# Shared expert rows added to the residual in DRAM during routing; the last stage loads two ranks at a time and adds two on VectorE

## The reference

```python
gate_w = ROUTED_SCALE * sel / sel.sum(-1, keepdims=True)      # top 8 of 64 experts per token
# each expert: (silu(xb @ Wg[e]) * (xb @ Wu[e])) @ Wd[e], on blocks of 128 (token, rank) pairs
routed = segment_sum(yb * row_w)                              # sum of the 8 ranks of a token
shared = (silu(t @ Sg) * (t @ Su)) @ w_shared_down
x = layer_norm(ALPHA * x1 + gate * (routed + shared)) * ln2_g + ln2_b
```

## Time and profile before

| what | value |
|---|---|
| median of 3 runs | 2107.01 us (2103.72 to 2113.51) |
| profiled execution | 2111.06 us |
| its span, first to last instruction | 2109.3 us |
| mean granted TensorE clock | 0.96 |
| PE busy | 1990.6 us, 94% |
| DVE busy | 1127.3 us, 53% |
| POOL busy | 541.9 us, 26% |

### The profile page before, as it was taken

One profiled execution on the slowest core, in us unless ns is written; L12 is line 12 of the kernel. 1 busy time (PEld: TensorE's weight loads), 2 busy tenths in 40 slices (PEclk: granted clock), 3 DMA queues, 4 the chain that ended last, 5 costly groups with the idle time before them and its releaser, 6 DMA issues. The chain is left out here.

```text
span 2109.3 us, 34455 instructions
## 1 busy us (share of the span) xinstructions
PE 1990.6 (94%) x8336; PEld 1392.6 (66%) x8337; DVE 1127.3 (53%) x1640; ACT 798.3 (38%) x1083; POOL 541.9 (26%) x676
## 2 busy tenths in 40 slices
PE   6999999999899989979999999999999999999785
PEld 1525545844797446447888888888888878888432
DVE  4102377211357455356755899743865882564166
ACT  0101111102113101125745788753865773565100
POOL 2000000000233222263333333322333332333144
PEclk9999999799599999999999999999999999999897
DMA  9350200000002234136774899844876793674586
GB/s 382 136 217 25 81 0 1 1 0 0 5 1 89 91 135 176 49 132 242 298 277 149 328 367 366 340 176 185 308 282 262 289 384 117 260 267 174 223 355 239
DMA packets 73623, 390.82 MB, mean 185 GB/s; under 512 B 20573, under 2 KB 20573, under 8 KB 54377
## 3 DMA queue, kind: packets, MB, share of 16 engines
q1 hardware_dynamic: 42104, 320.90, 39.5%
q0 software_dynamic: 31456, 69.27, 9.0%
q10 hardware_dynamic: 16, 0.03, 0.0%
HBM read 365.13 MB, written 73.69 MB: 208 GB/s over the span
## 5 line engine op out<-in xcount | busy, mean ns | idle before, releaser
L1654 DVE TENSOR_TENSOR split_weights<-raw_weights,split_weights (+1 forms) x384 | 448.2, 1219 | 27.4 <-ACT split_weights L629 22.8
L629 ACT ACTIVATE split_weights<-raw_weights (+1 forms) x384 | 380.7, 1063 | 9.7 <-issue 9.0
L1230 PE MATMUL psum<-split_weights,split_rows 128*128 (+1 forms) x864 | 347.6, 402 | 0.0
L629 ACT ACTIVATE arena<-psum 128x1024 f32<-128x1024 f32 (+3 forms) x202 | 164.1, 819 | 462.2 <-PE psum L1121 122.9
L1232 PE MATMUL psum<-split_weights,split_rows 128*128 (+1 forms) x864 | 337.8, 391 | 0.0
L1231 PE MATMUL psum<-split_weights,split_rows 128*128 (+1 forms) x864 | 336.6, 390 | 0.0
L629 ACT ACTIVATE split_rows<-psum 128x256 fp32r<-128x256 f32 (+1 forms) x217 | 154.0, 710 | 163.1 <-PE psum L1238 150.4
L1232 PEld LDWEIGHTS psum<-split_weights,split_rows 128*128 128x128 f32 x864 | 162.3, 188 | 35.9
L1231 PEld LDWEIGHTS psum<-split_weights,split_rows 128*128 128x128 f32 x864 | 162.8, 188 | 31.0
L1230 PEld LDWEIGHTS psum<-split_weights,split_rows 128*128 128x128 f32 x864 | 163.1, 189 | 30.0
L1249 PE MATMUL psum<-split_weights,split_rows 128*128 x432 | 168.9, 391 | 2.0 <-ACT arena L629 2.0
(11 more groups left out here) (243 smaller groups left out, 2713.0 us busy)
## 6 DMA issues: line engine op xcount, KB each, us to landing
raw_weights<-in_w_gu SPq DMA_DIRECT2D x64, 2048.0 KB, 9.2
raw_weights<-in_w_dn SPq DMA_DIRECT2D x64, 1024.0 KB
arena<-pair_rows SPq DMA_DIRECT2D x16, 2048.0 KB, 14.7
arena<-in_w_ada SPq DMA_DIRECT2D x12, 2048.0 KB, 9.4
arena<-in_toks SPq DMA_DIRECT2D x18, 512.0 KB, 9.5
arena<-in_w_vog SPq DMA_DIRECT2D x1, 4160.0 KB, 12.7
arena<-in_w_qk SPq DMA_DIRECT2D x1, 4096.0 KB, 18.4
arena<-in_w_out SPq DMA_DIRECT2D x2, 2048.0 KB, 7.9
```

The source lines that it names most:

```text
L629: return act.activation(o, i, ACT.Copy)
L1230: mm(bank(3 + p), xk, part(par, 0, 512 * k), start=(k == 0), stop=False)
L1654: tt(cols(wsplit, (1 - par) * (2 * WE) + (WE + 1024 * c), 1024), cols(raw, (1 - par) * WE + 1024 * c, 1024), high, ALU.subtract).then_inc( ...
```

## The change

The gate row is loaded once more early (`g2S`), divided by ALPHA on POOL and multiplied into both halves of `wsd`, so that the shared rows come out as gate times shared over ALPHA. PE's `shared_down` waits for that. The shared rows are still stored into `shared_rows`; then POOL issues, for each tile, an accumulating DMA from DRAM to DRAM (`add_shared`) that adds them to `x1_rows`. Three of these stand ahead of the one-hots, three among them (before numbers 24, 40 and 62), and two between the first two gathers' stores and the gather of block 2. SP waits for all eight before it loads x1. In the last stage the shared rows are no longer loaded, each tile comes in four loads of two ranks (1 MB each), POOL's `pair_sum` is gone, and DVE adds rank 6 to PE's sum and then rank 7. `acc_in` is called `yres`.

```diff
--- before.py
+++ after.py
@@ -261,6 +261,7 @@
         hTL = hTL.rearrange("p b (k n) -> p b k n", k=2)
         wsgu = at(A0 + 2048, 4096).rearrange("p (k n) -> p k n", k=8)
         wsd = at(A0 + 6144, 2048).rearrange("p (k n) -> p k n", k=2)
+        g2S = at(C0 + 19008, 1024)
 
         wsplit = overlay("split_weights", A0, 4 * WE, F32R)
         xg = at(4 * WE, 2 * XW).rearrange("p (b n) -> p b n", b=2)
@@ -277,7 +278,7 @@
 
         g2B, lg2, lb2 = (at(D0 - WE + i * 1024, 1024) for i in range(3))
         ybuf = [at(A0 + 1024 * i, 1024) for i in range(24)]
-        acc_in = [at(A0 + 24576 + 1024 * i, 1024) for i in range(8)]
+        yres = [at(A0 + 24576 + 1024 * i, 1024) for i in range(8)]
         PE_RANKS = 6
         assert A0 + 32768 <= D0 - WE
         x1_in = [at(D0 - WE + 4096 + 1024 * i, 1024) for i in range(8)]
@@ -394,6 +395,7 @@
                     sp.dma_start(wsgu, drows(a["w_shared_gu"], 0, 2 * DE)).then_inc(S("ws_in"), 16)
                 if j == 6:
                     sp.dma_start(wsd, a["w_shared_down"].rearrange("(p k) n -> p k n", k=2)).then_inc(S("ws_in"), 16)
+                    sp.dma_start(g2S, grow[3:4, :].to_broadcast([P, D])).then_inc(S("g2_in"), 16)
                 if j >= 1:
                     sp.wait_ge(S("ln_ready"), j)
                     sp.dma_start(t_dram[P * (j - 1):P * j, 0:D], lnt[:, (j - 1) % 2, :]).then_inc(S(f"t_out{(j - 1) % 2}"), 16)
@@ -432,7 +434,6 @@
                 sp.dma_start(shared_dram[P * j:P * j + P, :], yB[:, j % 2, :]).then_inc(S(f"acc_out{j % 2}"), 16)
             for i in range(2):
                 sp.wait_ge(S(f"acc_out{i}"), 16 * 4)
-                sp.wait_ge(S(f"x1_out{i}"), 16 * 4)
             sp.wait_ge(S("pad_out"), 16)
             with sp.Fori(1, NE // NBUF) as g:
                 for i in range(NBUF):
@@ -454,6 +455,7 @@
             sp.dma_start(g2B, grow[3:4, :].to_broadcast([P, D])).then_inc(S("rows2_in"), 16)
             sp.dma_start(lg2, a["ln2_g"].to_broadcast([P, D])).then_inc(S("rows2_in"), 16)
             sp.dma_start(lb2, a["ln2_b"].to_broadcast([P, D])).then_inc(S("rows2_in"), 16)
+            sp.wait_ge(S("x1_sum"), 16 * NTX)
             for j in range(NTX):
                 sp.dma_start(x1_in[j], x1_dram[P * j:P * j + P, :]).then_inc(S("rows2_in"), 16)
             sp.wait_ge(S("experts_done"), 1)
@@ -461,9 +463,8 @@
                 if j >= 3:
                     sp.wait_ge(S("ysum_pe"), j - 2)
                     sp.wait_ge(S("ysum_dve"), j - 2)
-                for h in range(2):
-                    sp.dma_start(at(A0 + 1024 * (TOPK * (j % 3) + 4 * h), 4096), pairs[P * j:P * j + P, 4096 * h:4096 * h + 4096]).then_inc(S(f"y_in{j % 3}{h}"), 16)
-                sp.dma_start(acc_in[j], shared_dram[P * j:P * j + P, :]).then_inc(S(f"accin{j % 3}"), 16)
+                for k in range(0, TOPK, 2):
+                    sp.dma_start(at(A0 + 1024 * (TOPK * (j % 3) + k), 2048), pairs[P * j:P * j + P, 1024 * k:1024 * k + 2048]).then_inc(S(f"y_in{j % 3}{k // 4}"), 16)
 
             for j in range(3):
                 load_pairs(j)
@@ -471,7 +472,7 @@
                 if j + 3 < NTX:
                     load_pairs(j + 3)
                 sp.wait_ge(S("out_ready"), j + 1)
-                sp.dma_start(out[P * j:P * j + P, :], acc_in[j]).then_inc(S("out_done"), 16)
+                sp.dma_start(out[P * j:P * j + P, :], yres[j]).then_inc(S("out_done"), 16)
             sp.wait_ge(S("out_done"), 16 * NTX)
 
 
@@ -542,11 +543,26 @@
                 if j >= 1:
                     rstd_of((S("x1_mv"), j), mvk[:, (j - 1) % 2, 1:2], 2 + (j - 1) % 2, "x1_rstd")
 
+            pool.wait_ge(S("ws_in"), 64)
+            pool.wait_ge(S("g2_in"), 16)
+            pool.tensor_scalar(g2S, g2S, 1.0 / ALPHA, None, ALU.mult).then_inc(S("prepared"), 1)
+            pool.wait_ge(S("prepared"), 1)
+            pool.tensor_tensor(wsd, wsd, g2S.unsqueeze(1).to_broadcast([P, 2, D]), ALU.mult).then_inc(S("prepared"), 1)
             pool.wait_ge(S("proj_done"), NTX)
-            pool.memset(at(4 * WE, 2 * XW), 0.0).then_inc(S("zpad_ready"), 1)
+            pool.memset(at(4 * WE, 2 * XW), 0.0).then_inc(S("prepared"), 1)
+
+            def add_shared(j):
+                pool.wait_ge(S(f"acc_out{j % 2}"), 16 * (j // 2 + 1))
+                pool.wait_ge(S(f"x1_out{j % 2}"), 16 * 4)
+                pool.dma_start(x1_dram[P * j:P * j + P, :], shared_dram[P * j:P * j + P, :], accum_op=ALU.add, max_dma_last_dim=4 * D).then_inc(S("x1_sum"), 16)
+
+            for j in range(3):
+                add_shared(j)
 
             pool.wait_ge(S("route_step"), SLOTS_READY)
             for q in range(64):
+                if q in (24, 40, 62):
+                    add_shared(3 + (24, 40, 62).index(q))
                 if q >= NOH:
                     pool.wait_ge(S("onehot_used"), q - NOH + 1)
                 pool.tensor_scalar(oneP[:, q % NOH], iota, p8[:, q:q + 1], None, ALU.is_equal).then_inc(S("onehotp_ready"), 1)
@@ -575,12 +591,14 @@
                 pool.indirect_dma_start(out=y_dram[0:NPAIR, :], out_offset=bass.IndirectOffsetOnAxis(ap=idxs[:, p:p + 1], axis=0),
                                         in_=yB[:, p], in_offset=None, bounds_check=NPAIR - 1, oob_is_err=False).then_inc(S(f"stored{p}"), 16)
 
-            pool.wait_ge(S("zpad_ready"), 1)
+            pool.wait_ge(S("prepared"), 3)
             gather(slice(0, 1), 0, 1)
             gather(slice(1, 2), 1, 2)
             for i in range(2):
                 pool.wait_ge(S(f"acc_out{i}"), 64)
                 pool.dma_start(y_dram[NPAIR + i:NPAIR + i + 1, :], cst[0:1, 0:D]).then_inc(S(f"stored{i}"), 16)
+            add_shared(6)
+            add_shared(7)
             pool.wait_ge(S("m_xb"), 1)
             gather(slice(2, 3), 0, 3)
             pool.wait_ge(S("m_xb"), 2)
@@ -605,18 +623,11 @@
                 pool.wait_ge(S("y_rstd"), NTX + j + 1)
                 pool.tensor_scalar(hst[:, j:j + 1], mv[:, 2 * j:2 * j + 1], rstd[:, j:j + 1], -1.0, ALU.mult, ALU.mult).then_inc(S("hrstd_ready"), 1)
 
-            def pair_sum(j):
-                pool.wait_ge(S(f"y_in{j % 3}1"), 16 * (j // 3 + 1))
-                y6, y7 = (ybuf[TOPK * (j % 3) + k] for k in (6, 7))
-                pool.tensor_tensor(y6, y6, y7, ALU.add).then_inc(S("og_ready"), 1)
-
             def final_gain(j):
                 pool.wait_ge(S("y_norm"), NTX + j + 1)
-                pool.tensor_tensor(acc_in[j], acc_in[j], lg2, ALU.mult).then_inc(S("y_gain"), 1)
+                pool.tensor_tensor(yres[j], yres[j], lg2, ALU.mult).then_inc(S("y_gain"), 1)
 
             for j in range(NTX + 1):
-                if j < NTX:
-                    pair_sum(j)
                 if 2 <= j < POOL_GAINS + 2:
                     final_gain(j - 2)
                 if j >= 1:
@@ -866,7 +877,7 @@
 
             for j in range(NTX):
                 act.wait_ge(S("hrstd_ready"), NTX + j + 1)
-                act.activation(acc_in[j], acc_in[j], ACT.Identity, scale=rstd[:, j:j + 1], bias=hst[:, j:j + 1]).then_inc(S("y_norm"), 1)
+                act.activation(yres[j], yres[j], ACT.Identity, scale=rstd[:, j:j + 1], bias=hst[:, j:j + 1]).then_inc(S("y_norm"), 1)
 
 
         @block.tensor
@@ -1143,6 +1154,7 @@
 
             def shared_down(j, slots=False):
                 pe.wait_ge(S("s_hx"), j + 1)
+                pe.wait_ge(S("prepared"), 2)
                 for k in range(2):
                     ins = pe.transpose(bank(7)[:, P * k:P * k + P], hxL[:, j % 2, k::2], ident)
                 ins.then_inc(S("sht_done"), 1)
@@ -1283,7 +1295,7 @@
 
                 for k in range(PE_RANKS):
                     if k % 4 == 0:
-                        pe.wait_ge(S(f"y_in{j % 3}{k // 4}"), 16 * (j // 3 + 1))
+                        pe.wait_ge(S(f"y_in{j % 3}{k // 4}"), 32 * (j // 3 + 1))
                     if j >= 2 and k == 0:
                         pe.wait_ge(S("ysum_read"), j - 1)
                     for h in range(2):
@@ -1694,14 +1706,13 @@
             dve.wait_ge(S("rows2_in"), 48 + 16 * NTX)
             for j in range(NTX + 2):
                 if j < NTX:
-                    y = acc_in[j]
-                    dve.wait_ge(S(f"accin{j % 3}"), 16 * (j // 3 + 1))
-                    dve.wait_ge(S("og_ready"), NTX + j + 1)
-                    tt(y, y, ybuf[TOPK * (j % 3) + 6], ALU.add).then_inc(S("ysum_dve"), 1)
+                    y = yres[j]
+                    dve.wait_ge(S("ysum_pe"), j + 1)
+                    dve.wait_ge(S(f"y_in{j % 3}1"), 32 * (j // 3 + 1))
+                    tt(y, psum[:, 0:1024] if j % 2 == 0 else psum[:, 1536:2560], ybuf[TOPK * (j % 3) + 6], ALU.add).then_inc(S("ysum_read"), 1)
+                    dve.wait_ge(S("ysum_read"), j + 1)
+                    tt(y, y, ybuf[TOPK * (j % 3) + 7], ALU.add).then_inc(S("ysum_dve"), 1)
                     dve.wait_ge(S("ysum_dve"), j + 1)
-                    dve.wait_ge(S("ysum_pe"), j + 1)
```

(6 more changed lines are left out.)

## The result

The changed kernel takes **2124.8 us** (median of 6 runs, 2119.8 to 2127.9) where the kernel before takes 2108.25 (6 runs, 2103.7 to 2113.5) on the same chip: 1.0075 times as long, with a 95% interval of 1.0055 to 1.0095. That is 16.5 us slower, with an interval of 11.6 to 20.0. The profiled execution after took 2122.33 for a span of 2120.5; the one before had 2111.06 and 2109.3. The spans differ by 11.2, and it is these 11.2 that can be placed row by row.

The account below looks back on a forecast made before the run. It took POOL's one-hots and tight first gathers to bound routing, and the store-load turn the last stage. 3.4 + 6.5 + 1.5 + 0.3 = 11.7 us on 2111.06 gave 2122.8 profiled, 2118.7 as a median, range 2108 to 2128.

Parts of the forecast that it names:

- Scaling: Before the first shared_down: POOL's two operations on w_shared_down take at most 7.0 us and end in time, costing 0.
- One-hot issues: Routing: add_shared 3 and 4 inside POOL's one-hots delay them 1.7 us each, 3.4 together (2.3 to 4.6).
- The third issue: Routing: add_shared 5 at q = 62 is covered by VectorE's other tables; without that cover it would cost 1.7 us.
- Gather 2: Routing: it queues behind two issues and the accumulations of tiles 6 and 7; delay 3.4 to 10.4 us, taken as 6.5.
- Half a gather's transfer for each 512 KB: Routing, data ahead of gather 2: low estimate of 3 us per accumulation, 6 for two; the high one was 12.
- the other estimate: Routing: the skill's fit of 2 us plus bytes over 436 GB/s, putting gather 2's delay under 6 us.
- Slower clock: PE behind the wait for gather 2: products run slower after the idle, adding 1.5 us (0 to 3).
- Last stage: Last stage: one more VectorE add behind PE, partly offset by dropping POOL's pair sum; +0.3 us (-1.5 to +2.5).
- Rival 2: Last stage: bytes bound it, so fewer bytes win 9.8 us there; kernel 4.1 faster, 2103; chance 0.10.
- Rival 1: Routing delays mostly hidden, clock stays up, last stage gives 1.5 us back; +4.2, 2111; chance 0.29.
- Rival 3: Routing: accumulations take 10 us each, gather 2 lands 18 late, later loads slip; +25, 2132; chance 0.11.

Follow-up runs that it names:

- thin67: Changed kernel with the accumulations of tiles 6 and 7 left in place but moving 128 of 1024 columns each; 2117.26 us, 1.0040 of the kernel before.
- copy67: Changed kernel with the transfers of tiles 6 and 7 copying instead of adding, same bytes and place; 2124.18 us, 1.0074 of the kernel before.
- late67: Changed kernel with the accumulations of tiles 6 and 7 moved behind gather 3; 2112.63 us, 1.0024 of the kernel before.
- no_load: Kernel before, with the last stage not loading the shared rows (left out of the result); 2106.94 us, 0.9985 of the kernel before.
- before_turns: Kernel before, with SP's loads running five tiles ahead of the stores instead of three; 2100.13 us, 0.9953 of the kernel before.
- after_turns: Changed kernel with SP's loads running five tiles ahead of the stores instead of three; 2106.91 us, 0.9992 of the kernel before.
- runs 10 and 11: after_turns and late67_turns, in this order; 2106.91 and 2093.02 us.
- late67_turns: Changed kernel with tiles 6 and 7's accumulations behind gather 3 and SP's loads five tiles ahead of the stores; 2093.02 us, 0.9923 of the kernel before.
- late67_turns5: As late67_turns, but PE sums five ranks and VectorE three; 2097.4 us, 0.9931 of the kernel before.

## Why the prediction was right, and where it wasn't

The direction, the place and the size were right: 2118.7 forecast, 2124.8 measured, within 2108 to 2128. By its own steps:

- **Scaling, 0.** Right. It took 8.4 in all, more than the 7.0 of two unblocked operations, and was still in time.
- **One-hot issues, 3.4 for two.** Too high, but near. An issue doesn't cost its duration plus the idle ahead of it, as I had added them: the next one-hot starts 0.63 after the DMA did. It costs more than these 0.63, though, as the one-hots behind it come slower. From the start of the third run of one-hots (897.75 in the earlier trace rows, 896.19 after) to the issue of gather 0 it is 32.4 to 32.5 in the six profiled executions without these three adds and 34.1 to 35.7 in the eight with them: 1.6 to 3.2 more, 2.6 in the mean, 1.7 in this execution. The other 0.6 of its +2.3 is gather 0, which PE had 11.22 after its issue instead of 10.66; that time is 10.2 to 11.2 in all executions. The third issue was mostly covered: the last one-hot product ends 2.6 later against the start of the third run, and 0.9 of that is gone by the issue of gather 0.
- **Gather 2, 6.5.** The mechanism was right, the size wasn't: +10.5, just over the 10.4 taken as the upper end. The three executions with both accumulations ahead of it have 25.5 to 26.0 between the first and third transposes, the nine without 15.2 to 16.3. The recorded step goes from accumulations that start at 950.5 and take 6 to 12 to a landing at 960.5 to 966.5, which holds another 4 for gather 2's own data without naming them. These 4 were right (its packets run 3.8), and the accumulations took the whole 12: 951.15 to 963.72. Half a gather's transfer for each 512 KB was too little, and the other estimate, 2.4 us of movement for both, far too little. Of the wait, 1.8 goes with two issues and 128 KB (thin67), about 2 with adding (copy67), the rest with the remaining bytes in the queue beside the weight loads.
- **Slower clock, 1.5.** The slower products are there: 0.63 instead of 0.40 up to 970.4, and 10.85 from the third transposes to the fourth instead of 9.43, 1.4 more. But the runs don't show that the stall brings them. In late67 and no_load, where PE waited only 0.79 and 0.76, the block took 11.05 and 11.03, with the same slow products at its start. So the step named something that happens here with and without the stall, and the kernel before happened to be profiled without it.
- **Last stage, +0.3.** Measured -0.5, within the scatter of 130.5 to 132.7. The recorded walk isn't added up rightly: for tile 7 its own terms, + 0.5, - 1.06 and + 1.25, give + 0.7 and not + 0.3. VectorE's order came as written: the last tile's moments 6.6 behind PE, L1712 never blocked, L1714 blocked to 1.97 beside POOL's gain. The Trainium skill ("SBUF — State Buffer", Who interferes with whom) says that a VectorE operation with two SBUF inputs contends with a GpSimd one that reads SBUF, and that one with at most one SBUF input doesn't, outside the 2-port modes, which an addition of two tensors hasn't got. The two rows of tile 3, beside one gain from 2040.22 to 2042.56, show just that. (In the earlier trace rows L1703 shows it less well: at 2018.96 it came after POOL's gain had ended.)
- **Rival 2, the bytes bounded the last stage.** Refuted by no_load: with 0.5 MB a tile less the stage is no shorter (133.1, one execution). The turn of store and load bounds it, and before_turns and after_turns show it by ending it. The prediction said that the turn counts; what it didn't ask is whether the turn had to be there.
- **Rival 1** fails by gather 2's 11.14. **Rival 3** had the idea of a slow accumulation. Its packets do take twice a copy's time, but copy67 is nearly as slow: it is the queue.

The sizes were off in opposite directions (one-hots, the stretch behind gather 2 and the last stage too high by 2.8 together, gather 2 too low by 4.0), and the sum, 11.7, ended close to the 12.8 that the steps measure without the chance of -1.6 upstream. That nearness is partly luck. The medians differ by 16.5; 12.8 lies within the interval of 11.6 to 20.0, and the 3.7 between the two stay open. The two lines moved in late67 are worth 12.2 in the medians there and 13.9 between runs 10 and 11, more than the 10.2 of the traces, so part of it may belong to gather 2.

## What to carry to other kernels

Put bulk transfers of a queue behind its latency-critical ones. Here 1 MB of software DMA ahead of a gather for which PE was already waiting 0.67 us cost 10, and moving two lines down got it back; how cheap its issue is (about 1 us) says nothing of that. And before counting saved bytes, look whether the loads wait for something else: 0.5 MB a tile was worth nothing while each load stood behind a store in program order, and over 6 us once it didn't.

## What was not expected of the hardware

- Issuing a 128-row DMA inside a stream of POOL operations holds up the next one by 0.63, though its row shows 0.85 to 0.95: the row overlaps the next operation. With the slower one-hots behind them, three issues cost 2.6 in this execution and 4.2 in late67_turns.
- Of two software transfers of 512 KB beside weight loads on the hardware queue, a copy landed after 12.0 and an accumulation after 14.5 (medians of two), where the six accumulations before took 5.0 to 7.2. The two queues moved equal numbers of packets (273 to 279, 187 to 186), so the one with packets of 4 KB got little more than a third of the bytes of the one with 8 and 16 KB.
- A packet of 4096 bytes takes 0.33 us as an accumulation from DRAM to DRAM and 0.16 as a copy.
- A VectorE add that reads PSUM kept its 1.22 beside POOL's 1024-element gain, while the next, with two SBUF inputs, went to 1.97, and to 3.25 in late67_turns5 with a longer overlap.
